# Experts by fours in 32-wide column tiles, whole-factor loads, and fused steps in the RMS norms

## The reference, cut to what matters

```python
lg = t @ w_rg + b_rg                       # 4 groups, the best one is taken
le_sel = ...                               # the 8 experts of that group
top_v, top_i = lax.top_k(le_sel, 2)        # 2 experts for each token
w = softmax(top_v) * wg
for e in range(32):
    hid = silu(t @ w1[e]) * (t @ w3[e])    # [1024 x 512] each
    y = y + comb[:, e:e + 1] * (hid @ w2[e])   # w2[e] is [512 x 1024]
```

```python
y = x * rsqrt(mean(x * x, axis=-1) + 1e-6) * g
```

## Time and profile before

| | us |
|---|---|
| median of 3 runs | 1644.99 (1643.57 to 1648.26) |
| the profiled execution's own time | 1647.44 |
| its span, first to last instruction | 1645.6 |
| PE busy | 1438.4 (87%) |
| PE weight loads busy | 1120.0 (68%) |
| DVE busy | 711.6 (43%) |
| ACT busy | 465.1 (28%) |
| all transfers | 374.07 MB, mean 227 GB/s |
| mean granted TensorE clock | 0.932 of 2.4 GHz |

### The profile page before, as it was taken

One profiled execution on the slowest core, in us unless ns is written; L12 is line 12 of the kernel. 1 busy time (PEld: TensorE's weight loads), 2 busy tenths in 40 slices (PEclk: granted clock), 3 DMA queues, 4 the chain that ended last, 5 costly groups with the idle time before them and its releaser, 6 DMA issues. The chain is left out here.

```text
span 1645.6 us, 21865 instructions
## 1 busy us (share of the span) xinstructions
PE 1438.4 (87%) x9454; PEld 1120.0 (68%) x9454; DVE 711.6 (43%) x1172; ACT 465.1 (28%) x653; POOL 1.9 (0%) x15
## 2 busy tenths in 40 slices
PE   6889886995999999999998859999798978799897
PEld 3679885884444444444444349999798878799897
DVE  3447983445101000100010154365637675578854
ACT  1433433322000000000000034344336443445442
POOL 0000000000000000000000000000000000000000
PEclk8999997996999999999999969999999998899999
DMA  9777513849899999999999237443254424255451
GB/s 321 272 245 248 157 64 114 270 165 373 302 366 376 378 390 390 379 377 369 379 389 395 80 95 229 133 133 124 77 166 129 129 92 151 91 178 181 154 189 43
DMA packets 223358, 374.07 MB, mean 227 GB/s; under 512 B 5767, under 2 KB 118809, under 8 KB 223129
## 3 DMA queue, kind: packets, MB, share of 16 engines
q1 hardware_dynamic: 223088, 369.04, 63.6%
q0 software_dynamic: 144, 3.54, 0.7%
q10 hardware_dynamic: 24, 0.03, 0.0%
HBM read 371.51 MB, written 4.62 MB: 229 GB/s over the span
## 5 line engine op out<-in xcount | busy, mean ns | idle before, releaser
L542 PE MATMUL bank<-fine 128*128 128x256 f32 x4656 | 594.0, 291 | 65.2 <-DVE fine L1134 65.1
L542 PEld LDWEIGHTS bank<-fine 128*128 128x128 f32 x4656 | 583.9, 199 | 75.2 <-issue 64.2
L1134 DVE TENSOR_TENSOR fine<-arena,fine 128x1024 fp32r<-128x1024 f32 (+1 forms) x261 | 302.8, 1191 | 204.3 <-ACT fine L1845 195.2
L1845 ACT ACTIVATE fine<-arena 128x1024 fp32r<-128x1024 f32 (+1 forms) x261 | 261.9, 1028 | 191.0 <-PE bank L542 124.5
L1845 ACT ACTIVATE arena<-bank 128x512 f32<-128x512 f32 (+2 forms) x189 | 88.8, 490 | 655.6 <-PE bank L810 185.0
L1134 DVE TENSOR_TENSOR arena<-arena,bank 128x512 f32<-128x512 f32 x16 | 11.0, 689 | 266.3 <-PE bank L810 266.2
L1845 ACT ACTIVATE arena<-arena 128x1024 f32<-128x1024 f32 (+6 forms) x93 | 65.1, 726 | 194.7 <-DVE arena L1134 98.4
L810 PE MATMUL bank<-arena 128*64 128x512 f32 x544 | 120.1, 594 | 0.0
L810 PE MATMUL bank<-above,arena 128*64 128x512 f32 x480 | 105.7, 594 | 0.0
L1142 DVE SCALAR_TENSOR_TENSOR arena<-arena 128x256 f32<-128x256 f32 (+2 forms) x261 | 105.4, 472 | 0.3
L1134 DVE TENSOR_TENSOR arena<-arena 128x512 f32<-128x512 f32 (+5 forms) x154 | 99.1, 666 | 9.4 <-ACT arena L1845 6.7
(11 more groups left out here) (157 smaller groups left out, 907.5 us busy)
## 6 DMA issues: line engine op xcount, KB each, us to landing
arena<-in_w SPq DMA_DIRECT2D x108, 1024.0 KB, 10.2
above<-in_w SPq DMA_DIRECT2D x84, 1024.0 KB, 9.8
arena<-in_w_in SPq DMA_DIRECT2D x62, 1024.0 KB, 5.5
arena<-in_w_ada SPq DMA_DIRECT2D x24, 1024.0 KB, 8.0
arena<-in_ffn_w_up SPq DMA_DIRECT2D x22, 1024.0 KB, 5.1
arena<-in_ffn_w_down SPq DMA_DIRECT2D x11, 1024.0 KB, 4.8
arena<-in_w_ada_f SPq DMA_DIRECT2D x8, 1024.0 KB, 8.9
arena<-in_w_gla_o SPq DMA_DIRECT2D x4, 1024.0 KB, 8.4
```

The source lines that it names most:

```text
L542: ins = e.matmul(o, w[:, k, j * P:j * P + P], x[:, kt, :], start=start, stop=stop, skip_group_check=True)
L1134: return e.tensor_tensor(o, a, b, f)
L1845: return e.activation(o, i, f, bias=bias, scale=scale)
```

## The change

`CAP` is 32 and four experts (a quad) are worked at a time: 8 quads, the same 128 slots in `xg`. Each up or down product has 32 slots of one expert (a tile of 128x32), the four experts in turn on the four column quarters of a bank. A slot holds one whole factor of one expert, [1024 x 512] or [512 x 1024], filled by one transfer of 2048 KB; there are 8 slots, the eighth made of the ring's last slot and the old place of `x`, where `xg` lay before (it has a place of its own now). A quad takes 12 slots; the four of one factor are released together. The general pass now starts above 32 tokens.

In the norms ScalarE squares all tiles, in pairs, each behind its own input, and TensorE sums behind each pair. At norms 0, 3 and 4 ScalarE writes `x_hi` straight from the normalised tile (scale and bias in one step) and VectorE `x_lo` with one fused step per tile (norm 0: two). At norm 2 VectorE writes the new h and ScalarE at the same time its squares for norm 3. Norm 2 stands before the first split of `q2`. The copy of `u` that later parts read is written by VectorE (norm 3: behind the pieces of `q2`).

The diff, cut to its core (renames of pair to quad and of `sent[15]` to `sent[7]` are left out):

```diff
-CAP = 64
+CAP = 32
...
-        xg = buf(2048, 2, 8, 128, at=xbase)
+        xg = buf(2048, 2, 8, 128)
...
-        wides = [above[:, WIDE * i:WIDE * i + WIDE] for i in range(FINE // WIDE)] + [arena[:, 0:WIDE]]
+        wides = [above[:, WIDE * i:WIDE * i + WIDE] for i in range(FINE // WIDE)] + [arena[:, 0:WIDE], arena[:, WIDE:2 * WIDE]]
...
-            n = 6 * pair + i
-            return n % NW, wides[n % NW].rearrange("p (e t n) -> p e t n", e=2, t=4 if i < 4 else 2), n
+            n = 12 * quad + i
+            return n % NW, wides[n % NW].rearrange("p (t n) -> p t n", t=8 if i < 8 else 4), n
...
-            def norm(i):
+            def norm(i, squares=sq):
                 bank = misc(rstd_a, i)
-                e.wait_ge(*sq_a[i])
                 for k in range(KT):
-                    if k == 4:
-                        e.wait_ge(*sq_v[i])
-                    ins = e.matmul(bank[:, 0:256], ones, sq[:, k, :], start=k == 0, stop=k == KT - 1)
+                    if k % 2 == 0:
+                        e.wait_ge(*sq_a[i, k // 2])
+                    ins = e.matmul(bank[:, 0:256], ones, squares[:, k, :], start=k == 0, stop=k == KT - 1)
...
-                    for th in range(2):
-                        s, slot, n = wide_of(pair, 2 * wn + th)
+                    for x in range(4):
+                        s, slot, n = wide_of(quad, 4 * wn + x)
                         e.wait_ge(*wide_in[s][n])
-                        if wn == 0:
-                            e.wait_ge(*gathered[pair, th])
-                        for k in range(4):
-                            for x in range(2):
-                                ins = e.matmul(bank[64 * x:64 * x + 64, :], xg[:, i, 4 * th + k, 64 * x:64 * x + 64],
-                                               slot[:, x, k, :], start=th == 0 and k == 0, stop=th == 1 and k == 3,
-                                               skip_group_check=True)
-                        ins.then_inc(*up_made.up((pair, 2 * wn + th)))
+                    for k in range(KT):
+                        if wn == 0 and k % 4 == 0:
+                            e.wait_ge(*gathered[quad, k // 4])
+                        for x in range(4):
+                            s, slot, n = wide_of(quad, 4 * wn + x)
+                            ins = e.matmul(bank[32 * x:32 * x + 32, :], xg[:, i, k, 32 * x:32 * x + 32], slot[:, k, :],
+                                           start=k == 0, stop=k == KT - 1, skip_group_check=True)
+                    ins.then_inc(*up_made.up((quad, wn)))
...
+                for k in range(4):
+                    for c in range(2):
+                        for x in range(4):
+                            s, slot, n = wide_of(quad, 8 + x)
+                            ins = e.matmul(ob[c][32 * x:32 * x + 32, :], hidT[:, i, k, 32 * x:32 * x + 32],
+                                           slot[:, k, 512 * c:512 * c + 512], start=k == 0, stop=k == 3, skip_group_check=True)
+                ins.then_inc(*down_made.up((quad, 0)))
...
+            def norm_split(i, name, g_col):
+                for k in range(KT):
+                    e.wait_ge(*normed[i, k // 4])
+                    e.wait_ge(*x_hi_a[name, "tile", k])
+                    ins = stt(x_lo[ph][:, k, :], sq[:, k, :], g_col(k), x_hi[ph][:, k, :].bitcast(F32), ALU.mult, ALU.subtract)
...
-            advance("q2", 1)
             e.wait_ge(*moe_h[7])
-            norm_rows(2, h)
             norm_apply(2, h)
-            norm_scale(2, lambda k: am[:, 16 + k:17 + k], lambda k: mod[:, 48 + k:49 + k], h)
-            e.wait_ge(*scaled_v[2, 6])
-            e.wait_ge(*scaled_a[2, 7])
-            norm_rows(3, h)
+            for k in range(KT):
+                if k % 4 == 0:
+                    e.wait_ge(*normed[2, k // 4])
+                ts(h[:, k, :], sq[:, k, :], am[:, 16 + k:17 + k], ALU.mult, mod[:, 48 + k:49 + k], ALU.add).then_inc(*scaled_v.up((2, k)))
+            advance("q2", 1)
+            e.wait_ge(*scaled_v[2, 7])
             norm_apply(3, h)
-            norm_scale(3, lambda k: col("ln1_g_2", k), None, u, "u2")
+            norm_split(3, "u2", lambda k: col("ln1_g_2", k))
             advance("q2", 4)
+            for k in range(KT):
+                ts(u[:, k, :], sq[:, k, :], col("ln1_g_2", k), ALU.mult).then_inc(*scaled_v.up((3, k)))
...
+            def norm_rows(i, ready):
+                for pair in range(4):
+                    e.wait_ge(*ready(pair))
+                    act(sq[:, 2 * pair:2 * pair + 2, :], h[:, 2 * pair:2 * pair + 2, :], ACT.Square).then_inc(*sq_a.up((i, pair)))
+                root(i)
...
+                    act(hi[:, k, :], sq[:, k, :], ACT.Identity, scale=scale_col(k), bias=shift_col(k) if shift_col else 0.0).then_inc(
+                        *x_hi_a.up((name, "tile", k)))
...
+            norm_rows(2, lambda pair: moe_h[2 * pair + 1])
             advance("q2", 1)
...
+                ins = act(u[:, k, :], sq[:, k, :], ACT.Square, scale=am[:, 16 + k:17 + k], bias=mod[:, 48 + k:49 + k])
...
-                for x in range(2):
-                    e.dma_start(slot[:, x, :, :], src[pair, :, x, kt * (i % 2):kt * (i % 2) + kt, :]).then_inc(
-                        *wide_in[s].up(n, 16))
+                e.dma_start(slot, (w1v, w3v, w2v)[i // 4][4 * quad + i % 4]).then_inc(*wide_in[s].up(n, 16))
```

More of the change, by code:

```diff
@@ L792, in gather_tokens @@
                             ins = e.matmul(bank[:, j * P:j * P + P], uT[:, tc, k * P:k * P + P],
-                                           hot2[:, tc, pair * P:pair * P + P], start=tc == 0, stop=tc == 1)
-                    ins.then_inc(*gather.up((pair, g)))
+                                           hot2[:, tc, quad * P:quad * P + P], start=tc == 0, stop=tc == 1)
+                    ins.then_inc(*gather.up((quad, g)))
             e.wait_ge(*uT_out[1, 1])
@@ L798, in tensor_program @@
             gather_tokens(0)
-            for pair in range(16):
-                i = pair % 2
+            for quad in range(8):
+                i = quad % 2
                 for wn in range(2):
-                    bank = take(wn, (silu_a, hid_v)[wn], pair)
-                    for th in range(2):
-                        s, slot, n = wide_of(pair, 2 * wn + th)
+                    bank = take(wn, (silu_a, hid_v)[wn], quad)
+                    for x in range(4):
+                        s, slot, n = wide_of(quad, 4 * wn + x)
@@ L839, in tensor_program @@
-                e.wait_ge(*send_out[pair])
+                ins.then_inc(*hid_turned.up(quad))
+                ob = [take(2 + n, (expert_a, expert_v)[n], ("ye", quad)) for n in range(2)]
+                e.wait_ge(*hidT_out[quad])
+                for x in range(4):
+                    s, slot, n = wide_of(quad, 8 + x)
+                    e.wait_ge(*wide_in[s][n])
+                for k in range(4):
+                    for c in range(2):
+                        for x in range(4):
+                            s, slot, n = wide_of(quad, 8 + x)
+                            ins = e.matmul(ob[c][32 * x:32 * x + 32, :], hidT[:, i, k, 32 * x:32 * x + 32],
+                                           slot[:, k, 512 * c:512 * c + 512], start=k == 0, stop=k == 3, skip_group_check=True)
@@ L854, in tensor_program @@
+                ins.then_inc(*sent.up(quad))
             e.wait_ge(*route["flag"])
@@ L904, in tensor_program @@
             norm(2)
-            norm(3)
+            norm(3, u)
             advance("q2", 4)
@@ L1295, in vector_program @@
             e.wait_ge(*mod_out["am0"])
-            norm_scale(0, lambda k: am[:, k:k + 1], lambda k: mod[:, k:k + 1], u, "u1")
+            for k in range(KT):
+                if k % 4 == 0:
+                    e.wait_ge(*normed[0, k // 4])
+                ts(u[:, k, :], sq[:, k, :], am[:, k:k + 1], ALU.mult, mod[:, k:k + 1], ALU.add).then_inc(*scaled_v.up((0, k)))
+                if k % 4 == 3:
+                    at = slice(k - 3, k + 1)
+                    e.wait_ge(*scaled_v[0, k])
+                    e.wait_ge(*x_hi_a["u1", "tile", k])
+                    tt(x_lo[0][:, at, :], u[:, at, :], x_hi[0][:, at, :].bitcast(F32), ALU.subtract).then_inc(*x_lo_v.up(("u1", k // 4)))
             advance("q", 2)
```

253 lines of the change are left out of this document (116 added, 137 removed).

## The result

The changed kernel takes 1587.66 us (median of 4 runs, 1587.24 to 1589.62) against 1646.30 for the kernel before in the same comparison: ratio 0.9647, 95% interval 0.9629 to 0.9665, 58.6 us less. The forecast was 1589. The profiled execution took 1587.45 us with a span of 1585.7.

What follows compares the result with a forecast made beforehand. TensorE was taken to pace the expert stage, transfers close behind. Savings of 37.6 + 13.9 + 3.8 + 1.5 + 0.4 = 57.2 us from the profiled 1647.44 gave 1590.2, stated as 1589; range 1579 to 1610.

Steps and rivals of the forecast that it cites:

- What bounds it: Expert stage: TensorE paces it before the change, transfers close behind; a pair of experts takes 32.9 us.
- (a) tiles: Expert stage: four 32-wide tiles work at once, 0.11 us an instruction; TensorE needs 32.7 us per four experts, not 65.8.
- rival 3: Expert stage: TensorE falls to half clock, a quad needs 58 us, still under 63.8; 1597 us; chance 0.08.
- (b) rate: Expert stage becomes bound by transfers at a mean of 394 GB/s, 63.8 us a quad; coarser release costs nothing.
- Rival 2: Expert-stage transfer rate stays lower: at 381 GB/s +16, so 1606 us; at 367 +34, 1624; chance 0.22.
- (c) start: Expert stage's start: up product at 411.8, transfers restart at 420.7, remaining 184.5 MB take 468.4 us, loads end at 889.1.
- (d) end: Expert stage's end: 15.2 us behind the last load, not 30.7; stage ends at 904.3 instead of 941.9, -37.6 us.
- (e) norms 2 and 3: Gap from the expert stage's end to the next projection: 23.1 us instead of 37.0, -13.9.
- (f) norms 4, 5 and 0: Norms outside the expert stage: norm 4 -3.8 us, norm 5 -1.5, norm 0 -0.4.
- The two large terms: Expert stage ending earlier, -37.6 us, and the shorter gap with norms 2 and 3 behind it, -13.9.
- The rival that ended slower: Expert stage: 32-wide tiles work only two at a time and at half clock, 100 us per quad; 1880 us; chance 0.03.
- The break-even: Expert stage: the kernel gets slower once a quad needs 7.1 us over 63.8, at 71 us.

Runs made afterwards that it cites:

- e6: Changed kernel with the quad's products reordered, two experts in turn and then the other two, down alike: 1597.91 us, ratio 0.9722.
- e8: Changed kernel with nine extra products, never read, right before the last down product: 1585.03 us, ratio 0.9635.
- e3: Changed kernel with each whole factor loaded in two transfers of 1024 KB: 1587.91 us, ratio 0.9651.
- e12: Changed kernel with norm 0's squares shared by ScalarE and VectorE as before, direct split kept: 1589.60 us, ratio 0.9662.
- e10: Changed kernel with the first four experts' masks made first and six extra products before the rank counts: 1585.44 us, ratio 0.9636.
- e1: Kernel before with only the expert part of the change, all six norms as before: 1609.66 us, ratio 0.9782.
- e2: Kernel before with the norm part of the change and a small reorder in the first block, experts in pairs: 1624.04 us, ratio 0.9867.
- e7: Changed kernel with the products of one expert after another, down alike: 1716.63 us (one run).
- e11: Changed kernel with masks first, extra products before rank counts, last w2 loads split, five extra products between last down product's halves: 1578.29 us, ratio 0.9592.

## Why the prediction was right, point by point

**What bounds it.** TensorE paced the stage before, transfers pace it after: 198 us of waits for loads where there were none, a quad every 63.9 us. e6 confirms it from the other side: it adds 100 us of TensorE's busy time to the stage and costs 10.

**(a) tiles.** 0.11 was taken, the rows at full clock give 0.107: the first 64 instructions run from 408.27 to 415.2. TensorE's clock fell all the same (0.78 in the mean, 0.50 in 440 to 444 behind a wait of 11 us, 1.00 again in 448 to 452), rival 3's condition in part, and it cost nothing within the stage, as that rival's sum said: only the last down product paid, 2.0 us (e8). The Trainium skill's "TensorE: Matmul & The Clock Gate" (HAM oscillation) says that a product behind a wait for loads starts cold, and the trace agrees: 0.50 behind the wait of 11 us.

**(b) rate.** 394 forecast, 394 measured, from 388 and 409 in two windows of the kernel before with a full queue. Rival 2 (the mean of 381 stays) is out; e3 had the same rate with transfers of half the size, so size was not what mattered. The figure of about 358 GB/s for one core in the Trainium skill, "DMA: Bandwidth & Descriptors" (Specifications), did not bind here either: even the 367 with 1 KB rows lies above it. Only one core was at work, so no run here says what two would get.

**(c) start.** The up product starts 43.2 us behind the first expert load, forecast 44.0; transfers restart 51.7 behind it, forecast 52.9; the loads end 520.7 behind it, forecast 521.3. Between the two the 184.5 MB took 469.0 us, forecast 468.4.

**(d) end.** 16.2 us, forecast 15.2: the landing, for which the forecast had no row, took 2.6 instead of 1, the down product 9.1 instead of 9.7 (at full clock it costs 7.1, e8), the rest 4.5 as forecast.

**(e) norms 2 and 3.** 14.5 instead of 13.9. The first sum ended at 5.4 as forecast; the second took 5.67 us, between its prices at full and at half clock, and ended 10.6 us after the first (forecast 11). One reading of the kernel before was not exact: its first sum started behind ScalarE's squares, as its row says, not behind VectorE's (951.71 to 952.93), which only its second half needs. Both stood behind a split of q2, so the step itself holds.

**(f) norms 4, 5 and 0.** Norm 4 gave 4.0 for 3.8. Norm 5 gave nothing where 1.5 was forecast: TensorE's sum starts at 1569.27, as before behind VectorE's last add, though three of the four pairs of squares are there by then.

```profile
1566.30 2.91 DVE L1137 TENSOR_TENSOR arena<-bank,arena 128x256 f32<-128x256 f32 x8 [7.04 <-PE bank L1117]
1567.09 2.79 ACT L1857 ACTIVATE arena<-arena 128x512 f32<-128x512 f32 x4 [9.09 <-DVE arena L1137]
1569.27 3.72 PE L597 MATMUL bank<-arena 128*128 128x256 f32 x16 [0.85 <-DVE arena L1137]
```

The step that failed there: I followed the squares and not the bank. The sum takes the next bank in turn, one of the four in which the down product stands, and such a bank is full until VectorE has added its last tile from it; TensorE waits for an add (0.85 us, from VectorE), the last one by its time (1569.21), and not for ScalarE. That reading rests on the code and this row; no run changed the bank. The forecast was too large in any case: TensorE is in the down product until 0.85 us before the sum, so no more than 0.85 was to be had. Norm 0 was put at 0.4, and as far as the profiles show it is worth some 1.2. The direct split gives 0.5: TensorE stands still before the first projection product for 7.59 us in the twelve kernels that have it and for 8.13 in the two that don't. The earlier first sum gives some 0.7 (e12 against e10); I had taken the loads of the modulation weights behind it for a full cover. The rest of the 2.8 us that the stretch lost is within what the clock does to kernels of the same code, whose first expert load comes at 363.2 to 367.9. The feed-forward's 1.8 us was not forecast. It comes with the norms: from the start of norm 4's sum to VectorE's first add of norm 5 it takes 215.5 us in the kernel before and in e1, and 209.6 to 209.9 in the changed kernel, e2, e3 and e12, of which 4.0 are norm 4's; its cause stays open.

So the total owes something to luck: the head (2.8 us where 0.4 were forecast) and the feed-forward (1.8 where none were) made up for norm 5 and more, and the profile's difference came to 59.9 us where 57.2 were forecast. The two large terms, 37.6 and 13.9, were met by 37.3 and 14.5 on the path that was forecast.

The rival that ended slower had the right mechanism and the wrong condition. In e7, where the order lets tiles overlap only at each change of expert, TensorE paces again and the kernel loses 4%. The break-even was put at 71 us a quad; as an estimate, it lies somewhat lower, since a slower TensorE also stretches both ends (e6: 11 us with nothing lost in between).

## What to carry to other kernels

When one engine paces a stage and the other stands at a share of 1 beside it, look for windows in the same trace in which the second one had a full queue: their rate, kind of transfer by kind, is what the stage will run at once the first is out of the way, and here it gave the stage within half a microsecond (errors of 0.6 to 1.2 us in its parts cancelled). From then on only what lies before the first release and behind the last landing costs time, so work there is worth splitting finely, while the middle can stay coarse as long as the other slots cover a release (here seven for groups of four, not six). Where a sum or product is to start earlier, follow its output bank as well as its inputs.

## What the runs showed of the hardware that was not expected

- With 32-wide tiles and one expert's products after another's, the mean was 0.363 us an instruction and not 0.43: products for a free tile start ahead of up to three that are still queued for a busy one (e7).
- The clock at the same point of the program differs between executions: with the same code, the first sum, 11 us into the program, took 3.69 to 6.11 us, and 16 short instructions 20 us later 1.95 to 3.58 us. The first expert load moved by 4.7 us with it. A single profile is no measure for steps of two us in the head, unless the durations of such instructions agree.
- Six extra products kept TensorE's clock up over a wait of 3.25 us for the ten short instructions of the rank counts, but not over the 1.67 us behind these: the gather ran in 6.4 us, and in 6.7 without them (e10, e11). Nine right before the down product did what was asked of them (e8).
